# A two-layer retention and sliding-window trunk: tensor work moves from GpSimd to VectorE, and 38 split weight pairs are kept in HBM

## What is computed

```python
SEQ, D_MODEL, CHUNK = 2048, 1024, 64          # all float32, batch 1
# layer 0: retention, 4 heads of key width 256 and value width 512
q, k, v, g = split(x @ w_in)                  # widths 1024, 1024, 2048, 2048
q, k = rope(q), rope(k) * 256 ** -0.5
inner = ((q_n @ k_n.T) * decay) @ v_n         # per head and chunk n
cross = (q_n @ state) * xi;  state = state * g_chunk + (k_n * zeta).T @ v_n
x1 = layer_norm(ALPHA * x + (silu(g) * group_norm(inner + cross)) @ w_out) * gain0 + bias0
# layer 1: 16 query heads on 4 key/value heads, each chunk sees itself and the one before
k, v = split(x1 @ w_kv);  q, gate = split(x1 @ w_in2)
p = softmax([q_n @ k_band.T / 8 + rel_bias, sink])
out = layer_norm(ALPHA * x1 + ((p @ v_band) * silu(gate)) @ w_out2) * gain1 + bias1
```

## Time and profile before

| | |
|---|---|
| median of 3 runs | 2687.63 us (2686.03 to 2691.45) |
| the profiled execution | 2693.96 us, its span 2692.2 us |
| busy: PE, DVE, ACT, POOL | 2392.4, 1985.4, 1153.4, 904.3 us |
| mean granted TensorE clock | 0.952 |
| HBM traffic | 411.92 MB of packets, 153 GB/s |

### The profile page before, as it was taken

One profiled execution on the slowest core, in us unless ns is written; L12 is line 12 of the kernel. 1 busy time (PEld: TensorE's weight loads), 2 busy tenths in 40 slices (PEclk: granted clock), 3 DMA queues, 4 the chain that ended last, 5 costly groups with the idle time before them and its releaser, 6 DMA issues.

```text
span 2692.2 us, 30949 instructions
## 1 busy us (share of the span) xinstructions
PE 2392.4 (89%) x11506; PEld 1932.7 (72%) x11506; DVE 1985.4 (74%) x2629; ACT 1153.4 (43%) x1422; POOL 904.3 (34%) x612
## 2 busy tenths in 40 slices
PE   5787779899979998999978999898997999899996
PEld 4665667687758777787767777677775877778775
DVE  7664667857896777875798676885789676778487
ACT  3332334434544444443544444453453444444353
POOL 5765652712362123320343222222136121332033
PEclk8988889999989999999989999999998999999998
DMA  9855744941434444644154433464244344354413
GB/s 312 296 203 190 267 144 157 329 124 63 152 128 133 128 156 141 196 132 124 65 171 150 141 126 126 148 221 126 76 133 134 118 149 150 101 168 153 126 56 109
DMA packets 206421, 411.92 MB, mean 153 GB/s; under 512 B 14080, under 2 KB 51472, under 8 KB 202688
## 3 DMA queue, kind: packets, MB, share of 16 engines
q1 hardware_dynamic: 194496, 354.60, 41.4%
q0 software_dynamic: 11776, 55.34, 5.7%
HBM read 360.87 MB, written 44.83 MB: 151 GB/s over the span
## 4 chain that ended last, share of the span: by engine, by line
PE 48%; DVE 22%; DMA 9%; issue 8%; POOL 7%; ACT 5%; SPq 0%; POOLq 0%; DVEq 0%; ACTq 0%
PE acc L567 13%; PE acc L568 12%; PE acc L569 12%; DVE w_lo L1155 7%; DMA stage<-t_prep 3%; ACT w_hi L853 3%; DMA t_prep<-t_buf 2%; DMA stage<-ret_w_in 2%; PE bank L567 2%; PE bank L568 2%; PE bank L569 2%; PE bank L771 2%; DVE q_tmp L1215 2%; PE bank L790 1%; PE bank L780 1%
## 5 line engine op out<-in xcount | busy, mean ns | idle before, releaser
L1155 DVE TENSOR_TENSOR w_lo<-stage,w_hi 128x1024 fp32r<-128x1024 f32 x536 | 768.1, 1443 | 447.0 <-ACT w_hi L853 440.9
L853 ACT ACTIVATE w_hi<-stage 128x1024 fp32r<-128x1024 f32 x536 | 561.5, 1056 | 636.7 <-PE acc L569 286.4
L567 PE MATMUL acc<-w_hi,xs 128*128 128x512 f32 x1120 | 463.0, 413 | 119.6 <-DVE w_lo L1155 61.8
L568 PE MATMUL acc<-w_lo,xs 128*128 128x512 f32 x1120 | 452.4, 404 | 0.0
L569 PE MATMUL acc<-w_hi,xs 128*128 128x512 f32 x1120 | 451.4, 403 | 0.0
L1600 POOL TENSOR_TENSOR rstd<-ve,half 128x1 f32<-128x1 f32 x96 | 59.5, 620 | 865.4 <-DVE ve L1196 553.4
L567 PEld LDWEIGHTS acc<-w_hi,xs 128*128 128x128 f32 x1120 | 220.0, 196 | 180.7 <-DVE w_lo L1155 71.3
L567 PE MATMUL acc<-x_hi,w_hi 128*128 128x512 f32 (+1 forms) x640 | 248.3, 388 | 9.2 <-ACT kT L1083 9.1
L569 PEld LDWEIGHTS acc<-w_hi,xs 128*128 128x128 f32 x1120 | 219.8, 196 | 49.0
L568 PEld LDWEIGHTS acc<-w_lo,xs 128*128 128x128 f32 x1120 | 220.5, 197 | 44.2
L568 PE MATMUL acc<-x_lo,w_hi 128*128 128x512 f32 (+1 forms) x640 | 239.4, 374 | 0.0
(11 more groups left out here) (186 smaller groups left out, 4570.2 us busy)
## 6 DMA issues: line engine op xcount, KB each, us to landing
stage<-t_prep SPq DMA_DIRECT2D x224, 512.0 KB, 4.1
stage<-ret_w_in SPq DMA_DIRECT2D x96, 512.0 KB, 4.0
stage<-ret_w_in SPq DMA_DIRECT2D x128, 256.0 KB, 3.0
stage<-swa_w_in SPq DMA_DIRECT2D x64, 512.0 KB, 3.8
t_prep<-t_buf POOLq DMA_DIRECT2D x24, 1024.0 KB, 5.1
stage<-ret_w_out SPq DMA_DIRECT2D x48, 512.0 KB, 3.7
cs<-rope_t SPq DMA_DIRECT2D x16, 1024.0 KB, 7.6
t_buf<-ret_w_in POOLq DMA_DIRECT2D x32, 512.0 KB, 8.8
```

The costliest lines, as they stand in the source:

```text
L567: mm(dst, lhs[0], rhs[0], start=start, stop=False, skip_group_check=reopened)
L568: mm(dst, lhs[0], rhs[1], start=False, stop=False, skip_group_check=reopened)
L853: copy(w_hi[:, g % HS], stage[:, g % LS], ACT.Copy).then_inc(w_hi_made, 1)
L1155: nc.vector.tensor_tensor(w_lo[:, g % LS], stage[:, g % LS], w_hi[:, g % HS].bitcast(F32), sub).then_inc(w_split, 1)
```

## The change

1. **T sets.** All 28 are made by DVE (`make_t` at the slots of the new table `T_PLAN`); POOL only loads them and stores them (`store_t`). SP no longer stores the first four.
2. **Keys.** `rope_k` goes to DVE, in two steps (`rope_k_products` straight from PSUM banks 2 and 3, ahead of `make_lo`; `rope_k_sums`). `rope_q` is cut into `rope_q_products` (one slot later) and `rope_q_sums` (two slots later).
3. **Sums.** ro's eight sums go to DVE (`ro_sum`, at the slots of `RO_SUMS`), three of so's four also, and one gate product of so. The x sums of the next block are made early: POOL loads quarters of x at slot G0 (`load_parts`, 2 MB), sums them at G0 + 2 (`sum_parts`) and stores them at G0 + 4 (`store_sums`); SP loads them at slot 3 of the next block, and they are split at slots VG + 1, + 2, + 4 and + 6 (before: slots 3 and 4).
4. **Second layer norm.** Both its pairs move to slots 0 and 1 of the next block; in the last block both stand behind the last product. `split_x` of the next block moves from slots SO + 9, SO + 10, 0, 1 to SO + 12, 0, 1, 2. The first turn of x1 moves from RO + 26 to RO + 27.
5. **Kept pairs.** For 38 pairs the split halves are stored in HBM (`keep`, 1 MB each) and in later blocks loaded ready-made, 1 MB each (`load_ready_made`, 3 slots ahead), so ACT and DVE skip them. Kept in block 0: the 4 qk pairs of head 0, the 12 of ro and 6 of so that belong to P1, P2 and P3. Kept in block 1: the 16 of vg that belong to P1 and P2. Buffers are reused only after their halves were stored (`wait_kept`).
6. **Accumulators.** One PSUM tensor `accs`, two counters (`x_free`, `y_free`); pairs of banks are emptied by one instruction of 1024 columns. The first product of pairs 0 and Q0 starts with banks 2 and 3; kv closes its values ahead of its last keys.
7. **Order in `after_retain`.** The next scores are evacuated ahead of `minus_mean`, which waits for POOL; `retain` of the fourth row tile comes half a pair later.

```diff
+KEPT_IN = {p: 0 for p in range(NP) if PAIRS[p][0] in ("ro", "so") and PAIRS[p][2] in RAW_B}
+KEPT_IN.update({p: 0 for p in range(VG)})
+KEPT_IN.update({p: 1 for p in range(NP) if PAIRS[p][0] == "vg" and PAIRS[p][2] in ("P1", "P2")})
...
+T_PLAN = [(0, 0, -1, 1), (1, 1, -1, 1), (2, 2, -1, 2), (3, 3, -1, 2), (4, 0, 6, 9), (5, 1, 6, 11), (6, 2, 7, 13),
+          (7, 3, 7, 16), (8, 0, 12, 17), (9, 1, 13, 20), (10, 2, 17, 20), (11, 3, 19, 21), (12, 1, 25, 31),
+          (13, 2, 28, 34), (14, 1, 35, 38), (15, 3, 30, 38), (16, 2, 37, 39), (17, 3, 42, 46), (18, 2, 45, 49),
+          (19, 3, 49, 52), (20, 2, 52, 55), (21, 3, 55, 57), (22, 3, 62, 65), (23, 3, 68, 70), (24, 4, 86, 102),
+          (25, 5, 88, 104), (26, 4, 104, 107), (27, 5, 106, 108)]   # set, buffer, slot of load, slot of make
...
+RO_SUMS = {67: "S3A", 70: "S3B", 71: "S2A", 73: "S4A", 74: "S1A", 79: "S2B", 81: "S1B", 83: "S4B"}
...
+            def load_ready_made(g):
+                if g >= NS * NP or not ready_made(g):
+                    return
+                p = g % NP
+                need(sp, products, used(g - HS))
+                wait_kept(sp, g - HS)
+                wait_kept(sp, g - LS)
+                wait_kept(sp, KEPT_IN[p] * NP + p)
+                sp.dma_start(w_hi[:, g % HS].bitcast(F32), w_cache[KEPT.index(p), 0]).then_inc(w_loaded[g % LS], 16)
+                sp.dma_start(w_lo[:, g % LS].bitcast(F32), w_cache[KEPT.index(p), 1]).then_inc(w_loaded[g % LS], 16)
+            def keep(g):
+                if to_keep(g):
+                    n = KEPT.index(g % NP)
+                    sp.wait_ge(w_split, SPLITS[g])
+                    sp.dma_start(w_cache[n, 0], w_hi[:, g % HS].bitcast(F32)).then_inc(w_kept[g % LS], 16)
+                    sp.dma_start(w_cache[n, 1], w_lo[:, g % LS].bitcast(F32)).then_inc(w_kept[g % LS], 16)
...
             for s in range(NS):
                 for p in range(NP):
+                    load_ready_made(s * NP + p + AHEAD)
                     load_pair(s * NP + p + LOAD_AHEAD)
+                    keep(s * NP + p)
...
+            def rope_k_products(H):
+                s, h = divmod(H, RH)
+                dve.wait_ge(products, full(s, h * HEAD + 3, 3))
+                dve.wait_ge(rope_loaded, 16 * (H + 1))
+                need(dve, r_full, 4 * H)
+                need(dve, scored, 4 * H)
+                mark(nc.vector.tensor_tensor(k_tmp[:], accs[:, 2:4, :], both(3), ALU.mult))
+                nc.vector.tensor_tensor(krT[:], accs[:, 2:4, :], both(2), ALU.mult).then_inc(y_free, 2)
...
                     if p == NP - 1 and s == NS - 1:
+                        ln_pair(s, 1, 0)
                         ln_pair(s, 1, 2)
+                    if s == 0:
+                        for n, _, _, at_slot in T_PLAN:
+                            if at_slot == p:
+                                make_t(n)
...
+            def sum_parts(s):
+                pool.wait_ge(parts_loaded, 64 * s)
+                a11, s3, a12, s2 = (x[:] for x in parts)
+                link(tt(s3, a11, s3, sub))
+                link(tt(s2, s2, s3, sub))
+                tt(a11, s2, a11, add)
+                tt(a12, a12, s2, sub).then_inc(parts_summed, 1)
...
+                    if p < 2 and s > 0:
+                        ln_pair(s - 1, 1, 2 * p)
...
+                    if s + 1 < NS:
+                        if p == G0:
+                            load_parts(s + 1)
+                        if p == G0 + 2:
+                            sum_parts(s + 1)
+                        if p == G0 + 4:
+                            store_sums(s + 1)
```

More of the change, by code:

```diff
@@ L87, in bank_of @@
     return j if q in IN_X else 2 + j
[L90 to L95, removed]
+X_BANKS, Y_BANKS = 0, 1
+FILLS = [[p for p, (_, _, q, i) in enumerate(PAIRS) if i == 0 and (q is None or (q in IN_X) == (c == X_BANKS))]
+         for c in range(2)]
 def prior(s, p, m):
-    return s * len(FILLS[m]) + FILLS[m].index(p)
+    c = m // 2
+    n = FILLS[c].index(p)
+    in_turn = PAIRS[FILLS[c][n - 1]][0] not in ("q", "qk")
+    return 2 * (s * len(FILLS[c]) + n) - int(in_turn and m % 2 == 0)
 def emptied(s, p, m):
-    return prior(s, p, m) + 1
+    c = m // 2
+    return 2 * (s * len(FILLS[c]) + FILLS[c].index(p)) + m % 2 + 1
 def first_pair(kind, h, q):
@@ L702, in kv_block @@
                         pe.wait_ge(x1_split, 8 * s + 6 + k // 4 + 1)
-                    done = [values(3, k), keys(0, 1, k), keys(1, 1, k)]
+                    mm = values(3, k)
+                mm.then_inc(products, 1)
+                for k in range(KD):
+                    done = [keys(0, 1, k), keys(1, 1, k)]
                     if k == KD - 1:
@@ L943, in copy_r @@
                     if s == 0:
[L944 removed]
+                        wait_stored(act, last_set(h))
                     elif h < 2:
@@ L979, in _ @@
                         make_hi(g + AHEAD)
+                    if p < 3 and s > 0:
+                        split_x(s, 1 + p)
                     if p < 2 and s > 0:
-                        split_x(s, 2 + p)
+                        norm_z(s - 1, 1, 2 * p)
+                        norm_z(s - 1, 1, 2 * p + 1)
                     if h < RH and j < VG:
@@ L995, in _ @@
                         if j == 3:
[L996 removed]
                             need(act, scored, 4 * H)
[L998 to L1000 removed]
+                            act.wait_ge(products, full(s, p, 1))
+                            copy(qrT[:], accs[:, 0:2, :], ACT.Copy).then_inc(x_free, 2)
                     if h < RH and j >= VG:
@@ L1010, in _ @@
                                 need(act, stored, 64 * s)
-                                act.wait_ge(xs_split, 4 * (s + 1))
+                            if H == 0:
+                                act.wait_ge(xs_split, 4)
                             need(act, dstate_full, 8 * H)
-                            for i in range(2):
-                                empty(s, p, i, v_raw[:, i, :]).then_inc(acc_free[i], 1)
-                        if v == 2:
+                            act.wait_ge(products, full(s, p, 1))
+                            copy(v_raw[:, 0:2, :], accs[:, 0:2, :], ACT.Copy).then_inc(x_free, 2)
+                        if v == 3:
                             act.wait_ge(q_roped, H + 1)
@@ L1031, in _ @@
                             state_to_hi(H, 0)
-                            for i in range(2):
-                                empty(s, p, i, sg[:, i, :]).then_inc(acc_free[i], 1)
+                            act.wait_ge(products, full(s, p, 1))
+                            copy(sg[:, 0:2, :], accs[:, 0:2, :], ACT.Copy).then_inc(x_free, 2)
                         if v == 8:
@@ L1300, in output_sums @@
                             dve.wait_ge(res_loaded[t], 16 * (s + 1))
-                        onto_z(s, first + n - 1, "P1", t, 0)
+                    onto_z(s, first + n - 1, "P1", 0, 0)
                 if i == 2 * n:
-                    for t in range(2):
-                        more_z(s, first + 2 * n - 1, "P2", "P1", t, 0)
+                    more_z(s, first + 2 * n - 1, "P2", "P1", 0, 0)
                 if i == 2 * n + 1:
@@ L1308, in output_sums @@
                 if i == 3 * n:
-                    for t in range(2):
-                        onto_z(s, first + 3 * n - 1, "P6", t, 1)
+                    onto_z(s, first + 3 * n - 1, "P6", 0, 1)
                 if i == 4 * n:
@@ L1644, in _ @@
                 pool.wait_ge(x_loaded[w], 16)
-            for n in range(T_EARLY):
+            for n in range(4):
                 load_t(n)
```

545 lines of the change are left out of this document (275 added, 270 removed).

## The result

The changed kernel takes **2763.35 us** (median of 4 runs, 2756.2 to 2774.0) against 2686.83 us for the kernel before beside it: ratio 1.0285, 95% interval 1.0249 to 1.0321. It is slower by 77 us where the forecast said 160 faster; the range ended at 2605. The profiled execution took 2763.92 us, its span 2762.1.

The account below looks back on a forecast made before the run. PE, busy 2392 of 2692 us, was the bound; its idle time and half-clock stretches could be won. Block gains 79.5, 23, 29 and 29, together 160.5 us, gave 2533.5 profiled, 2527 us as median; range 2475 to 2605.

Parts of the forecast that it names:

- The rope and P6 in blocks 1 to 3: Heads 1 to 3 there: gains of 1, 1.5 and 6.5 us in block 1, then 2.5, 2.5 and 8.
- ro and so of block 0: Block 0's output stages: ro gains 8 us (bounds -10 to +20), so gains none as stores meet loads of x.
- head 0 of block 0: First head of the first block: a gain of 8 us, with bounds of -8 (slower) to +18.
- Rival (e): Slower than before: a kept pair's load comes late, losing from a landing of 14.3 us; 2708 us at 15; chance 0.03.
- rival (b): Transfers at the rate: 86 kept pairs' loads cost 0.4 to 0.5 us each, 40 us, giving 2567 us; chance 0.09.
- kv, q and ro: Projection and retention output stages: kv and q gain 2 us a block (1.5 in block 0), ro 6 in blocks 1 to 3.
- Head 0 of blocks 1 to 3: First head after each block border: gain 8 us in block 1, 10 in blocks 2 and 3; bounds 2 and 16.
- The gate stage: Unit 7's division waits behind `sum_parts` in POOL's queue: loss of 5 us in blocks 0 to 2, from 0 to 10.
- rival (c): POOL against the softmax: gate stage loses 10 us, not 5, head 0 gains 3 less in three blocks: 2551 us; chance 0.10.
- The tail: End of the last block: `ln_pair` for tiles 0 and 1 follows the last product, loss 5 us, from 3 to 7.
- DVE in block 0's heads: Heads 1 to 3 of block 0: DVE's added work just fits; gains of 31, 25 and 11 us.
- rival (a): DVE becomes the bound: block 0's three heads win only half, the four first heads nothing: 2596 us; chance 0.13.

Follow-up runs that it names:

- experiment 1: The changed kernel with part 5 undone, so no split pair is stored or read back: 2596.25 us (ratio 0.9647).
- 5: The changed kernel with kv's copies of `kT` and `vt` put ahead of the split of pair 106 on both engines: 2760.66 us (ratio 1.0255).
- 6: The changed kernel with the four additions of `sum_parts` spread, one behind each division of slots 114 and 115: 2770.21 us (ratio 1.0284).
- 10: The changed kernel without part 5, kv emptied first, x splits a slot earlier, x sums' additions waiting for pair 104's end: 2550.60 us.
- 9: The changed kernel without part 5, kv emptied first, x splits a slot earlier, x sums loaded in slot 105, added in 107: 2559.66 us.

## Why the prediction was wrong, step by step

**The step that failed** is in the paragraph "The rope and P6 in blocks 1 to 3": kept pairs "instead add 4 MB of stores to four pairs, about 1 us late per head". It priced the bytes and left out the waits on the landing (`wait_kept`, ahead of the next load and of the next `w_hi`) and their places in SyncE's queue, although the diff shows them and the earlier trace rows has 5.1 us for a store of 1 MB. Working it out would have taken one line: no second store before the first has landed gives at least 5.1 + 0.4 us a stored pair against 2.9 us of products, 2.6 us late each, 100 us over 38 pairs. The runs show 7.3 us from store to store in block 1's head 1 and 4.0 us lost per stored pair (experiment 1). The same term was missing in ro and so of block 0 (+8 and 0 forecast; -23 and -16.5 measured, with 12 and 6 stored pairs) and in head 0 of block 0, where the bounds of -8 to +18 did not hold the measured -23. SyncE's queue there, after:

```profile
35.94 2.92 SPq L501 DMA_DIRECT2D w_cache<-w_lo  x1
56.47 0.38 SPq L481 DMA_DIRECT2D stage<-ret_w_in  x1
...
67.68 0.77 PE L625 MATMUL accs<-w_hi,xs 128*128 128x512 f32 x1 [33.87 <-ACT qrT L1071]
```

There are 20.5 us from one store to the next load, and PE idles 33.9 us at pair 4 (up to 67.7 us): ScalarE's copy of `qrT`, which ends that wait, stands behind splits that waited 24.75 and 6.11 us for landed stores. TensorE then works at a granted clock of 0.50 from 67.7 to 72.2 us, where a product of 512 columns takes 0.63 us; from 72.8 us on it takes 0.40.

**Rival (e)** had the right sign, the right part and the wrong transfer. It let the *load* of a kept pair come late; those land after 3.6 and 4.7 us, and PE waited for them twice, 2.3 us in all. It was the store that was late, in blocks 0 and 1. With so few waits for loads, rival (b) did not come true in this form either.

**kv, q and ro.** "2 a block" for kv and q was -13.0 in block 1 (26.9 + 51.4 to 36.0 + 55.3). There are two errors. PE's wait at pair 104, 2.1 us before, was to go and is 6.5 to 7.0 us, because the emptying of kv stands behind `make_hi(106)`; with the emptying first (5) 3.1 to 3.6 us of it go in blocks 1 to 3 and 1.1 in block 0. That `make_hi(106)` itself comes later because the keys are closed later is read from the code and was not tested. And the turn of x1 one pair later did not hide `ln_pair`: ro is 9.2 us shorter and kv 9.1 longer in block 1, and without part 5 PE still waits 2.4 us for `z` and 2.1 to 3.0 for `x_lo` at pair 100. The work and its wait went over the border between two stages, so ro's 6 us were not there to be won.

**Head 0 of blocks 1 to 3.** The waits at pairs 2 and 3 came as forecast (0.8 and 3.9 us in block 2 with ready weights, 5.0 and 3.8 without). 6.5 and 7.1 us were won in blocks 2 and 3 for 10 forecast.

**The gate stage** lost 6.8, 5.5, 5.4 and 0 us in blocks 0 to 3 for 5, 5, 5 and 0 forecast, with PE's wait of 3.9 to 4.3 us at the division, as worked out from GpSimd's queue; rival (c)'s 10 us did not come. The Trainium skill ("SBUF — State Buffer", "Who interferes with whom") says that a VectorE instruction with two SBUF inputs contends with a GpSimd instruction that reads SBUF; the trace of 6 agrees (0.70 to 2.12 us). **The tail** lost 3.6 us for 5.

**DVE in block 0's heads** was right (31, 25, 11 forecast; 34.5, 21.6, 10.9), so rival (a) fell: DVE is busy 68.9 of 83.3 us in head 1.

**The account**, by profiled spans: 230 us lie between the forecast (2692.2 - 160.5 = 2531.7) and 2762.1. Of these 171 are part 5 (experiment 1; 167 by medians). Without it the change gains 101 of the 160 (95 by medians): 42 are missing in ro, kv and q, 33 in the four blocks' heads 0, and the other heads and so gave some 16 more than forecast.

Left open are the last 13 us of the stores, and why reading ready pairs costs head 3 and so of the later blocks time. The traces show where: in block 2's head 3 PE's longest gap, ahead of a product with `att_hi`, is 4.8 us (1.5 without part 5), and in its so the waits for `z` are 4.2 and 1.3 us (2.4 and none over 1). Not tried was issuing the stores from another engine's queue, where no load of weights stands behind them.

## What to carry to other kernels

Price a new transfer by its waits before its bytes: who waits for its landing, and what stands behind that wait in the issuing engine's queue; if the next transfer of its kind is among it, they run one at a time. Judge each part of a change on the kernel as the other parts leave it: work taken off an engine that the other parts had already relieved was worth nothing here. Where GpSimd and VectorE share the chip, place GpSimd's work by a wait on the progress that it must follow (q 51.6 us in 10, 55.4 in 9), not by its line in a program.

## What the runs showed of the hardware

Of the two stores of 512 KB of a pair, issued 0.5 us apart, the second lands 6.3 us after its issue (median of 38; 7.6 with two pairs under way, 5.0 with three):

```profile
w_cache<-w_hi SPq DMA_DIRECT2D x38, 512.0 KB, 5.6
w_cache<-w_lo SPq DMA_DIRECT2D x38, 512.0 KB, 6.3
```

That is with slices of up to 426 GB/s between 895 and 940 us. In the first 60 us of the kernel, with the DMA share of head 0 at 0.85, one took about 20 us (issued at 35.94, the load that waits for it at 56.47). The Trainium skill ("DMA: Bandwidth & Descriptors", "Anatomy of one DMA — SWDGE (gpsimd) path") says that a wait on a semaphore is spent in the issuing sequencer and not in the DMA engines; SyncE's 158.4 us of waits at L371, beside slices of 0 to 51 GB/s, agree.

A VectorE copy with one SBUF input was stretched by GpSimd's additions as much as a two-input one: 0.28 to 2.44 us, and 0.36 to 2.19, while the copy out of PSUM kept 1.2. Rival (c) priced two-input steps alone. The Trainium skill ("SBUF — State Buffer", "Who interferes with whom") lists copies among the operations that can take the ports that VectorE shares with GpSimd; the trace agrees, with those numbers.
